# The second block's projection of p moved to the gap between the FFN and that block, and the residuals done on VectorE alone

## The chip, the cores and the metric

The kernel runs on one core of one Trainium2 chip, in one launch. The metric is device time in microseconds: the median of three runs of the kernel before is 2093.15 us (2092.73, 2093.15 and 2098.65). The profile comes from another execution, which took 2099.14 us.

## What is computed

The input is one sequence of 256 tokens with 2048 features; all arithmetic is float32. The first block is an RWKV-7 mixer followed by a convolutional FFN, both under adaptive modulation; the second block is windowed attention beside a short convolution, followed by a gate on a projection of a second input `p` (256 features a token). What matters here, cut from the reference:

```
y, v_first = _rwkv7_mix(h, ...)                       # ends in y @ w_o
x = x + g_m * _rms(y, norm_mix_post)                  # residual 1
h = _rms(x, norm_ffn_pre) * (1 + sc_f) + sh_f
f = _conv_ffn(h, ...)                                 # ends in @ w_out
x = x + g_f * _rms(f, norm_ffn_post)                  # residual 3
# second block
z = rms_norm(x, norm_gain) @ w_in                     # q, k, v, gates, convolution
x = x + mix @ w_out
gate = sigmoid(rms_norm(x, ple_gate_norm_gain) @ w_ple_gate + b_ple_gate)
e = rms_norm(p @ w_ple_proj, ple_norm_gain)           # reads neither x nor z
x = x + gate * e
```

`e` depends on `p` and its weights alone, so `p @ w_ple_proj` can be computed at any time before the last line.

## The kernel before

**Layout.** Activations lie feature-major: 16 tiles (`NT`) of 128 features by 256 tokens (`S`). The residual stream is `xr`, 2 MB.

**Split matmuls.** Every weight tile from `wo` on is split into a high and a low part. ScalarE copies a half unit of weights to `whi` (`hi_part`, L1225), VectorE subtracts to get `wlo` (`lo_part`, L1674), and TensorE multiplies (`split_tiles`, L713 high weights by high and low activations, 512 columns; L714 low weights by high activations, 256 columns). A tile of output takes 16 such pairs. `part_out` (L1232, ScalarE) and `join` (L1682, or L1740 with a scale, VectorE) add the two halves of the bank. Four PSUM banks (0 to 3) take turns; banks 4 to 7 are for side work.

**Phases and the weight ring.** `PHASES` lists the phases in order; here they are `wo` (16 tiles), `fi` (86), `fo` (16, each of three weight units), `zk` (12: keys, queries, values), `zg` (8), `zc` (32), `zo` (16) and `pg` (16). SyncE loads the weight units of 1 MB, in this order, into a ring of four slots; a slot is loaded again when the unit that lay in it is released, which for a split unit is when VectorE has made its low part (`released`).

**Order.** All engines run an order written out by hand and wait on semaphores that count. Each engine and each DMA queue is in order.

**Stage A, from `wo` to `fi`.** TensorE sums the squares of y over partitions (`rms(1)`, L672), ScalarE takes the root (`root`, L1200), VectorE the reciprocal (`rec`, L1714). `residual(1, ...)` then multiplies y by it (four pieces of 128x1024, L1723) and adds it to `xr` (L1727). Pieces 2 and 3 of the multiplication are GpSimd's (`scale_y`, L612); VectorE waits for them (`res_pool`). ScalarE squares each piece of the new x (`squares`, L1194), TensorE sums the squares (16 matmuls, L677), root and reciprocal follow. The new x is multiplied by that (pieces 0 and 1 on VectorE, L1959; 2 and 3 on GpSimd, L618), ScalarE applies scale and shift (L1454), and `split_x` makes high (L1707) and low part (L1708) of each piece. TensorE starts the first half of `fi` when two pieces are split (`x_lo`), and its second half when all four are.

**Stage B, from `fo` to `zk`.** The same residual as `residual(3, ...)`, with x read back from memory into `xy`. ScalarE makes the high part of each of 16 tiles (`scaled_hi`, L1506), VectorE the low part (`scaled_lo`, L1748). TensorE starts the first half of the first tile of `zk` when the low parts 0 to 7 are there, and the second with all 16. ScalarE squares x in four pieces (L1513), GpSimd adds them up (L640, three additions), and TensorE sums over partitions (`after_zk(0)`, L1070) after the first tile of `zk`; root, reciprocal and the scaling of `zk`'s tiles follow, and from the third tile on TensorE does side work for the heads (L1062, L1082).

**Stage C, `zo`.** When the last step of `zc` is done, GpSimd issues two loads of 1 MB, the weights of `p`'s projection, to `wp` (L644), whose place is in use until then. After each of the first eight tiles of `zo` TensorE does a pair of tiles of `p @ w_ple_proj` (8 matmul instructions in the trace, L1163, into bank 4 or 5) in `after_zo`. ScalarE squares the pair (L1615) and copies it to `ee` (L1616), GpSimd adds the squares to `esum`; after tile 9 TensorE sums them, and VectorE scales `ee` in `zo`'s tiles 11 to 14.

Of the kernel before, what the change touches and what calls it, by code (L numbers as in the profile page):

```python
# [29 lines left out]
F32 = mybir.dt.float32  # L30
# [32 lines left out]
          ("zk", 12, 12, 24, 1), ("zg", 8, 8, 16, 1), ("zc", 32, 32, 64, 1),  # L63
# [105 lines left out]
def build(nc, t, out, stage=99, dbg=None):  # L169
    with ExitStack() as ctx:  # L170
# [73 lines left out]
        wp = place("wp", 120, [P, 2, 2048])  # L244
# [85 lines left out]
        res_pool = sem("res_pool")  # L330
        xn_pool = sem("xn_pool")
        zsq_sum = sem("zsq_sum")
        ld_wp = sem("ld_wp")
        e_mm = sem("e_mm")
        e_ev = sem("e_ev")
# [98 lines left out]
        def _(sp):  # L434
# [35 lines left out]
            for name, nu, _, ns, split in PHASES:  # L470
                for k in range(nu):
                    released[RV_UNIT.get((name, k), UNIT[name] + k)] = (w_lo, HALF[name] + 2 * k + 2) if split else \
                        (ada_used, ADA_REST + k + 1) if name == "ada" else (pe_step, STEP[name] + (k + 1) * ns // nu)
# [61 lines left out]
            sp.dma_start(pt[:].rearrange("p i s -> p (i s)"), t["p"]).then_inc(ld_p, 16)  # L535
            stream("zk", t["zin"][0:12], 12)
# [13 lines left out]
        def _(pool):  # L550
# [57 lines left out]
            def scale_y(k, y):  # L608

                pool.wait_ge(rms_rec, k + 1)  # L610
                for q in (2, 3):
                    nc.gpsimd.tensor_tensor(y(q), y(q), rms_rs.unsqueeze(1).to_broadcast([P, 4, S]),  # L612
                                            ALU.mult).then_inc(res_pool, 1)

            scale_y(1, lambda q: cum[:, 4 * q:4 * q + 4, :])
            pool.wait_ge(rms_rec, 3)
            for q in (2, 3):
                nc.gpsimd.tensor_tensor(h[:, 4 * q:4 * q + 4, :], xr[:, 4 * q:4 * q + 4, :],  # L618
                                        rms_rs.unsqueeze(1).to_broadcast([P, 4, S]), ALU.mult).then_inc(xn_pool, 1)

# [14 lines left out]
            scale_y(3, lambda q: xy[:, q, 1])  # L635
# [7 lines left out]
            for k in range(2):  # L643
                pool.dma_start(wp[:, k, :], t["wp"][k]).then_inc(ld_wp, 16)  # L644
            for i in range(NT):
                for e in range(2 * i, 2 * i + 2 if i < 8 else 2 * i):
                    pool.wait_ge(e_ev, i + 1)
# [14 lines left out]
        def _(pe):  # L662
# [58 lines left out]
            def project_split(name, x2, n, between=None, x_rdy=()):  # L721

                def one(k, it):
                    bank_free(TILE[name] + k, it)
                    for x in range(2):
# [3 lines left out]
                        split_tiles(slot, 8, x2, 8 * x, (TILE[name] + k) % BANKS, x == 0, x == 1).then_inc(pe_step, 1)  # L729

# [334 lines left out]

            def after_zk(k):
                if k == 0:
                    pe.wait_ge(zsq_sum, 3)
# [3 lines left out]
                    m.then_inc(rms_sum, 1)  # L1072
                for e in new_heads(k):
# [10 lines left out]
            project_split("zk", x2, 12, after_zk, ((x_lo, 6), (x_lo, 8)))  # L1084
# [66 lines left out]
            def after_zo(k):  # L1151

                if k < 8:
                    if k == 0:
                        pe.wait_ge(ld_wp, 32)
                        pe.wait_ge(ld_p, 16)
                    elif k >= 2:
                        pe.wait_ge(e_ev, k - 1)
                    for e in range(2):
                        i = 2 * k + e  # L1160
                        w = wp[:, i // 8, :].rearrange("p (q m) -> p q m", q=2)
                        for q in range(2):
                            m = mm(ps[:, 4 + k % 2, e * S:(e + 1) * S], w[:, q, (i % 8) * P:(i % 8 + 1) * P], pt[:, q, :],  # L1163
                                   start=q == 0, stop=q == 1)
                    m.then_inc(e_mm, 1)
# [14 lines left out]
        def _(act):  # L1180
# [270 lines left out]
            for i in range(NT):  # L1451
                if i % 4 == 0:
                    act.wait_ge(*((xn_rdy, i // 4 + 1) if i < 8 else (xn_pool, i // 4 - 1)))
# [801 lines left out]
```

## Time and profile before

| | us |
|---|---|
| runs | 2098.65, 2093.15, 2092.73 |
| median | 2093.15 |
| profiled execution | 2099.14 |
| its span, first to last instruction | 2097.5 |
| TensorE matmul busy | 1967.6 (94% of the span) |
| VectorE busy | 1391.2 (66%) |
| ScalarE busy | 896.4 (43%) |
| GpSimd busy | 144.4 (7%) |
| mean granted TensorE clock | 0.968 |
| chain that ended last | TensorE 90%, VectorE 5%, DMA 3% |

The busy shares are means over stages that have different limits. The chain that ended last is followed back from the last instruction; the granted clock is a share of full speed, 1.00 for 2.4 GHz and 0.50 for 1.2 GHz. Where TensorE has nothing to do, a row of another engine stands in the chain. The stages of the change lie at 755 to 797 us (A), 1521 to 1571 us (B) and 1891 to 1960 us (C).

### The profile page before, as it was taken

Reading aid. Unit: us, or ns where it says so; the run is one execution under the profiler, and the core shown is the slowest. Engines: PE = TensorE matmul, PEld = TensorE weight load, DVE = VectorE, ACT = ScalarE, POOL = GpSimd, SP = SyncE. Lnnn points to the kernel's source line nnn. Section 1 sums busy time; section 2 is a strip of 40 time slices with the busy share of each in tenths; the row PEclk is TensorE's granted clock in tenths of the full one; section 3 lists DMA queues with packets and bytes.
Section 4 is the critical chain, followed back from the end, with each engine's and each line's share of the span. In section 5 each row is a group of like instructions: output and inputs, shape, how many; then the busy total and the mean of one; then the engine's idle time right before and its main releaser. Section 6 shows DMA issues by size and latency. Waiting matters only on the chain.

```text
span 2097.5 us, 34270 instructions
## 1 busy us (share of the span) xinstructions
PE 1967.6 (94%) x13392; PEld 1708.1 (81%) x13392; DVE 1391.2 (66%) x1975; ACT 896.4 (43%) x1457; POOL 144.4 (7%) x126
## 2 busy tenths in 40 slices
PE   3999999898998959999999999999959999999999
PEld 2888888787886848888888888888848888887887
DVE  5985459544847977777777776444466567764676
ACT  2335221031333535555555555444444445544553
POOL 2000002000002330000000000000030000002200
PEclk8999999899999979999999999999979999999999
DMA  9986324576645924555555556555524435444453
GB/s 403 413 323 209 121 85 157 201 276 260 243 179 200 409 103 181 193 186 180 185 191 184 182 187 228 184 181 192 192 80 161 161 141 189 153 153 174 158 199 121
DMA packets 58790, 415.14 MB, mean 198 GB/s; under 512 B 6528, under 2 KB 6656, under 8 KB 12416
## 3 DMA queue, kind: packets, MB, share of 16 engines
q1 hardware_dynamic: 54368, 382.24, 49.6%
q0 software_dynamic: 4032, 27.26, 3.3%
q10 hardware_dynamic: 288, 4.19, 0.5%
q8 instruction: 74, 1.21, 0.2%
q14 instruction: 28, 0.23, 0.0%
HBM read 409.48 MB, written 4.19 MB: 197 GB/s over the span
## 4 chain that ended last, share of the span: by engine, by line
PE 90%; DVE 5%; DMA 3%; issue 1%; ACT 1%; POOL 1%; SPq 0%; DVEq 0%; POOLq 0%; ACTq 0%
PE ps L713 41%; PE ps L714 20%; PE ps L690 12%; PE ps L792 4%; PE ps L786 1%; PE ps L772 1%; DMA ring<-in_wv 1%; PE ps L763 1%; DMA bk<-in_ada 1%; PE ps L1163 1%; PE ps L1018 1%; PE ps L808 1%; DVE ring L1652 1%; PE ps L945 1%; POOL zsq L640 1%
## 5 line engine op out<-in xcount | busy, mean ns | idle before, releaser
L713 PE MATMUL ps<-x_pair,whi 128*128 128x512 f32 x2464 | 878.7, 401 | 30.1 <-issue 17.2
L714 PE MATMUL ps<-x_pair,wlo 128*128 128x256 f32 x2464 | 692.8, 281 | 0.0
L1674 DVE TENSOR_TENSOR wlo<-ring,whi 128x1024 fp32r<-128x1024 f32 x468 | 548.2, 1208 | 105.6 <-ACT whi L1225 101.6
L713 PEld LDWEIGHTS ps<-x_pair,whi 128*128 128x128 f32 x2464 | 464.5, 188 | 149.7 <-issue 37.4
L1225 ACT ACTIVATE whi<-ring 128x1024 fp32r<-128x1024 f32 x468 | 462.4, 1031 | 99.7 <-PE ps L714 99.6
L714 PEld LDWEIGHTS ps<-x_pair,wlo 128*128 128x128 f32 x2464 | 467.1, 190 | 0.3
L1232 ACT ACTIVATE px<-ps 128x256 f32<-128x256 f32 x202 | 77.8, 385 | 500.0 <-PE ps L714 500.0
L713 PE MATMUL ps<-hid_pair,whi 128*128 128x512 f32 x688 | 243.3, 399 | 0.0
L714 PE MATMUL ps<-hid_pair,wlo 128*128 128x256 f32 x688 | 193.2, 281 | 0.0
L690 PE MATMUL ps<-mixb,ring 128*128 128x256 f32 x640 | 148.0, 394 | 13.9 <-DMA ring<-in_wv 12.4
L713 PEld LDWEIGHTS ps<-hid_pair,whi 128*128 128x128 f32 x688 | 129.3, 188 | 32.6 <-DVE wlo L1674 0.3
L690 PEld LDWEIGHTS ps<-mixb,ring 128*128 128x128 f32 x640 | 125.9, 198 | 33.7 <-DMA ring<-in_wv 13.4
L1652 DVE CUSTOM_DVE_ANT_0 ring<-ring,cb,prm 128x2048 f32<-128x2048 f32 x42 | 97.6, 2349 | 83.6 <-DMA ring<-in_ada 82.8
L714 PEld LDWEIGHTS ps<-hid_pair,wlo 128*128 128x128 f32 x688 | 130.0, 189 | 0.0
L1682 DVE TENSOR_TENSOR px<-ps,px 128x256 f32<-128x256 f32 x134 | 56.4, 421 | 99.1 <-ACT px L1232 98.8
L690 PE MATMUL ps<-mixa,ring 128*128 128x256 f32 x512 | 115.3, 388 | 0.0
L690 PEld LDWEIGHTS ps<-mixa,ring 128*128 128x128 f32 x512 | 99.3, 195 | 14.4 <-issue 0.2
L1740 DVE TENSOR_TENSOR px<-ps,px 128x256 f32<-128x256 f32 x68 | 28.9, 425 | 122.2 <-ACT px L1232 122.1
L1989 DVE SCALAR_TENSOR_TENSOR tmp<-px,prm,tmp 128x255 f32<-128x255 f32 x86 | 41.6, 484 | 81.5 <-ACT tmp L1478 81.5
L713 PE MATMUL ps<-y_pair,whi 128*128 128x512 f32 x256 | 90.7, 399 | 2.5 <-DVE h L1921 1.4
L792 PE MATMUL ps<-mixb,ring 128*128 128x256 f32 x384 | 85.9, 380 | 0.0
L1478 ACT ACTIVATE tmp<-px,prm 128x256 f32<-128x256 f32 x86 | 51.8, 602 | 70.0 <-DVE px L1682 70.0
(294 smaller groups left out, 2320.5 us busy)
## 6 DMA issues: line engine op xcount, KB each, us to landing
ring<-in_fi SPq DMA_DIRECT2D x86, 1024.0 KB, 4.8
ring<-in_zin SPq DMA_DIRECT2D x52, 1024.0 KB, 4.8
ring<-in_ada SPq DMA_DIRECT2D x42, 1024.0 KB, 6.8
ring<-in_fo SPq DMA_DIRECT2D x32, 1024.0 KB, 4.8
bk<-in_ada SPq DMA_DIRECT2D x22, 1024.0 KB, 10.7
ring<-in_wr SPq DMA_DIRECT2D x16, 1024.0 KB, 4.8
ring<-in_wv SPq DMA_DIRECT2D x16, 1024.0 KB, 4.9
ring<-in_wo SPq DMA_DIRECT2D x16, 1024.0 KB, 8.9
```

The lines of the kernel that those rows point to most:

```text
L690: last = mm(ps[0:m, bank, 0:S], w[:, k * m:(k + 1) * m], act[:, k, :], start=k == 0, stop=k == n - 1)
L713: mm(ps[:, bank, 0:2 * S], w_h, pair_k, start=first and k == 0, stop=False)
L714: m = mm(ps[:, bank, 0:S], w_l, pair_k[:, 0, :], start=False, stop=last and k == n - 1)
L792: last = mm(outer_bank(m), ring[:, i % RING, m * P:(m + 1) * P], mixb[:, i, :], start=i == 0 and m % 2 == 0, stop=i == NT - 1, skip_group_ ...
L1225: A(whi[:, hf % WB, 0:m], ring[:, u % RING, 1024 * x:1024 * x + m], ACT.Copy).then_inc(w_hi, 1)
L1232: A(part[:, (TILE[name] + k) % 4, :], ps[:, (TILE[name] + k) % BANKS, S:2 * S], ACT.Copy).then_inc(x_part, 1)
L1478: A(tmp[:, (k % 4) * S:(k % 4 + 1) * S], join_in("fi", k, it), ACT.Identity, scale=param_at("fcw", 4 * FT, kk), bias=param_at("fcb", 0, kk ...
L1652: V.tensor_tensor_reduce(out=w, in0=w, in1=cb[:], scale=1.0, scalar=prm[:, m:m + 1], op0=ALU.mult, op1=ALU.add, accum_out=mod[:, m:m + 1]) ...
L1674: V.tensor_tensor(wlo[:, hf % WB, 0:m], ring[:, u % RING, 1024 * x:1024 * x + m], whi[:, hf % WB, 0:m].bitcast(F32), ALU.subtract).then_in ...
L1682: return V.tensor_tensor(o, ps[:, (TILE[name] + k) % BANKS, 0:S], o, ALU.add).then_inc(joined, 1)
L1740: own(V.tensor_tensor(o, ps[:, (TILE[name] + k) % BANKS, 0:S], o, ALU.add))
L1989: own(V.scalar_tensor_tensor(d[:, 1:S], b[:, 0:S - 1], param_at("fcw", 2 * FT, kk), d[:, 1:S], ALU.mult, ALU.add))
```

## The change

- The projection of `p` (its eight pairs of tiles) is done around the start of `zk`: pairs 0 to 4 ahead of `zk`, pairs 5 and 6 between the two halves of its first tile (`first_half`), pair 7 after that tile. Three banks (4 to 6) take turns instead of two. The sum of x's squares moves from after `zk`'s first tile to after its second.
- Its weights are two more units of SyncE's ring, phase `pp`, ahead of `zk`; they are released after pair 3 and pair 7. GpSimd's loads of `wp` are gone.
- ScalarE copies each pair to `ee_0` (`p_out`); the whole of it is stored to memory (`spill_e`, 2 MB) in `zk`'s step 1 and loaded by GpSimd to `ee` when `zc` is done. In `zo` ScalarE squares `ee`.
- The pieces of both residuals and of the normalization behind the first that GpSimd did are VectorE's. The splits are in two halves: in A three pieces are normalized, two split, then the fourth normalized and two split; in B three pieces are added, low parts 0 to 7 made, then the fourth added and low parts 8 to 15 made (before: two pieces, four low parts, then the rest).

```diff
-          ("zk", 12, 12, 24, 1), ...
+          ("pp", 2, 0, 0, 0), ("zk", 12, 12, 24, 1), ...
-        wp = place("wp", 120, [P, 2, 2048])
+        ee_0 = place("ee_0", 108, [P, NT, S])
@@ SyncE
-                        (ada_used, ...) if name == "ada" else (pe_step, ...)
+                        (ada_used, ...) if name == "ada" else (e_mm, 4 * k + 4) if name == "pp" else (pe_step, ...)
+            few("pp", [t["wp"][k] for k in range(2)])
             stream("zk", t["zin"][0:12], 12)
@@ GpSimd
-            scale_y(1, lambda q: cum[:, 4 * q:4 * q + 4, :])
-            pool.wait_ge(rms_rec, 3)
-            for q in (2, 3):
-                nc.gpsimd.tensor_tensor(h[:, 4 * q:4 * q + 4, :], xr[:, 4 * q:4 * q + 4, :],
-                                        rms_rs.unsqueeze(1).to_broadcast([P, 4, S]), ALU.mult).then_inc(xn_pool, 1)
-            scale_y(3, lambda q: xy[:, q, 1])
             pool.wait_ge(pe_step, STEP["zo"])
-            for k in range(2):
-                pool.dma_start(wp[:, k, :], t["wp"][k]).then_inc(ld_wp, 16)
+            pool.wait_ge(e_spill, 16)
+            pool.dma_start(ee[:].rearrange("p i s -> p (i s)"), t["spill_e"]).then_inc(ld_e, 16)
@@ TensorE
+                        if first_half and k == 0 and x == 0:
+                            first_half()
+            def p_pair(k):
+                u = UNIT["pp"] + k // 4
+                if k % 4 == 0:
+                    unit_in(u)
+                if k >= 3:
+                    pe.wait_ge(e_ev, k - 2)
+                for e in range(2):
+                    i = 2 * k + e
+                    w = ring[:, u % RING].rearrange("p (q m) -> p q m", q=2)
+                    for q in range(2):
+                        m = mm(ps[:, 4 + k % 3, e * S:(e + 1) * S], w[:, q, (i % 8) * P:(i % 8 + 1) * P], pt[:, q, :],
+                               start=q == 0, stop=q == 1)
+                m.then_inc(e_mm, 1)
             def after_zk(k):
                 if k == 0:
+                    p_pair(7)
+                elif k == 1:
                     pe.wait_ge(zsq_sum, 3)
                     ...
+                if k == 2:
+                    pe.wait_ge(e_ev, 8)
-            project_split("zk", x2, 12, after_zk, ((x_lo, 6), (x_lo, 8)))
+            pe.wait_ge(ld_p, 16)
+            for k in range(5):
+                p_pair(k)
+            def two_pairs():
+                p_pair(5)
+                p_pair(6)
+            project_split("zk", x2, 12, after_zk, ((x_lo, 6), (x_lo, 8)), two_pairs)
             def after_zo(k):
-                if k < 8:
-                    ...
@@ ScalarE
+            def p_out(k):
+                act.wait_ge(e_mm, k + 1)
+                A(ee_0[:, 2 * k:2 * k + 2, :]..., ps[:, 4 + k % 3, :], ACT.Copy).then_inc(e_ev, 1)
+            p_out(0)
             hi_part("zk", 1)
-            for i in range(NT):
-                if i % 4 == 0:
-                    act.wait_ge(x_done, NT + i + 4)
-                scaled_hi(i, "n2")
+            for q in range(4):
+                p_out(q + 1)
+                act.wait_ge(x_done, NT + 4 * q + 4)
+                for i in range(4 * q, 4 * q + 4):
+                    scaled_hi(i, "n2")
             for q in range(4):
                 A(zsq[:, q, :], ..., ACT.Square).then_inc(rms_sq[4], 1)
+                if q < 2:
+                    p_out(5 + q)
@@ in zk's step 1
+                    p_out(7)
+                    act.wait_ge(e_ev, 8)
+                    act.dma_start(t["spill_e"], ee_0[:].rearrange("p i s -> p (i s)")).then_inc(e_spill, 16)
                     root(4)
@@ in zo's steps 1 to 8
-                    act.wait_ge(e_mm, k)
-                    if k >= 3:
+                    if k == 1:
+                        act.wait_ge(ld_e, 16)
+                    elif k >= 3:
                         act.wait_ge(e_acc, 2 * (k - 2))
-                    A(esq[:, (k - 1) % 2], b, ACT.Square)
-                    A(ee[:, 2 * k - 2:2 * k, :], b, ACT.Copy).then_inc(e_ev, 1)
+                    A(esq[:, (k - 1) % 2], ee[:, 2 * k - 2:2 * k, :], ACT.Square).then_inc(e_sq, 1)
@@ VectorE, residual
-                    if q < 2:
-                        V.tensor_tensor(y(q), y(q), ..., ALU.mult).then_inc(sprd, 1)
-                        dve.wait_ge(sprd, 2 * done + q + 1)
-                    else:
-                        dve.wait_ge(res_pool, 2 * done + q - 1)
+                    V.tensor_tensor(y(q), y(q), ..., ALU.mult).then_inc(sprd, 1)
+                    dve.wait_ge(sprd, 4 * done + q + 1)
                     V.tensor_tensor(xr[:, 4 * q:4 * q + 4, :], x(q), y(q), ALU.add).then_inc(x_done, 4)
-                    if q == 1 and k == 3:
+                    if q >= 2 and k == 3:
                         yield
@@ VectorE, from residual 1 to fi
-            for q in range(2):
-                V.tensor_tensor(h...)
-            split_x(h, xhi, xlo, h_rdy, 1 * NT, x_lo)
+            for q in range(3):
+                xn(q)
+            split_x(h, xhi, xlo, h_rdy, 1 * NT, x_lo, (0, 1))
+            xn(3)
+            split_x(h, xhi, xlo, h_rdy, 1 * NT, x_lo, (2, 3))
@@ VectorE, from residual 3 to zk
-            next(halves)
-            for i in range(4):
+            next(parts)
+            for i in range(8):
                 scaled_lo(i, "n2", 0)
-            next(halves)
-            for i in range(4, NT):
+            next(parts)
+            next(parts)
+            for i in range(8, NT):
                 scaled_lo(i, "n2", 0)
```

## Rows read from the trace of the kernel before

**Rows 1.** Waits of TensorE: engine, line, releaser: total us, times, longest us.
```profile
PE ps L677 <- ACT mixb L1194: 24.9, 3, 16.1
...
PE ps L713 <- DVE x_pair L1708: 13.0, 1, 13.0
...
PE ps L1070 <- POOL zsq L640: 6.2, 1, 6.2
...
PE ps L1163 <- DMA wp<-in_wp: 3.2, 1, 3.2
```

**Rows 2.** Chain that ended last, 745 to 800 us: start, us, what.
```profile
759.01 1.24 DVE cum L1723
...
760.34 3.17 DVE mixa L1727
...
768.16 1.06 ACT mixb L1194
...
769.27 7.78 PE ps L677 x24
...
779.36 4.51 DVE h L1959 x2
783.87 2.76 DVE x_pair L1707
...
787.89 0.61 DVE x_pair L1707
```

**Rows 3.** Windows of TensorE: us, busy (instructions), granted clock, DMA share, GB/s.
```profile
764.60:768.50 3.90, 3.78 (x8) 0.50 0.01 2
...
773.00:775.00 2.00, 2.00 (x9) 0.75 0.00 0
...
1545.30:1548.00 2.70, 2.70 (x17) 0.98 0.00 0
```

**Rows 4.** The same chain, 1510 to 1580 us.
```profile
1527.43 1.24 DVE xy L1723
...
1539.30 3.30 ACT x_pair L1506 x8
...
1544.58 5.23 POOL zsq L640
...
1555.62 3.67 PE ps L1070 x8
...
1570.59 0.34 PE ps L1062 x4
```

**Rows 5.** Timelines of single engines, 1500 to 1560 us: start, us, engine, line, operation, [idle before].
```profile
1540.44 4.84 DVE L1748 SCALAR_TENSOR_TENSOR x_pair<-mixa,prm,x_pair 128x256 fp32r<-128x256 f32 x12
...
1544.58 10.99 POOL L640 TENSOR_TENSOR zsq<-zsq 128x1024 f32<-128x1024 f32 x3 [10.44 <-ACT zsq L1513]
...
1542.21 0.77 PE L713 MATMUL ps<-x_pair,whi 128*128 128x512 f32 x1 [17.18 <-issue]
```

**Rows 6.** The same chain, whole span, stretch of zo.
```profile
1901.52 3.78 PE ps L1163 x8
1911.86 1.73 PE ps L1163 x8
...
1955.93 1.73 PE ps L1163 x8
```

**Rows 7.** Timeline of ScalarE, 1890 to 1960 us.
```profile
1905.83 0.59 ACT L1616 ACTIVATE ee<-ps 128x512 f32<-128x512 f32 x1
...
1912.18 2.00 ACT L1225 ACTIVATE whi<-ring 128x1024 fp32r<-128x1024 f32 x2
```

**Rows 8.** DMA issues, 1870 to 1960 us: KB, median us to landing.
```profile
wp<-in_wp POOLq DMA_DIRECT2D x2, 1024.0 KB, 8.1
```

**Rows 9.** DMA issues, 780 to 810 us.
```profile
spill<-mixa ACTq DMA_DIRECT2D x1, 2048.0 KB, 6.2
```

**Rows 10.** DMA issues, 1500 to 1560 us.
```profile
ring<-in_zin SPq DMA_DIRECT2D x6, 1024.0 KB, 4.8
```

More of the change, by code:

```diff
@@ L62 @@
           ("wo", NT, NT, 2 * NT, 1), ("fi", 2 * FT, 2 * FT, 4 * FT, 1), ("fo", 3 * NT, NT, 6 * NT, 1),
-          ("zk", 12, 12, 24, 1), ("zg", 8, 8, 16, 1), ("zc", 32, 32, 64, 1),
+          ("pp", 2, 0, 0, 0), ("zk", 12, 12, 24, 1), ("zg", 8, 8, 16, 1), ("zc", 32, 32, 64, 1),
           ("zo", NT, NT, 2 * NT, 1), ("pg", NT, NT, 2 * NT, 1)]
@@ L329, in build @@
         x_hi = sem("x_hi")
-        res_pool = sem("res_pool")
-        xn_pool = sem("xn_pool")
         zsq_sum = sem("zsq_sum")
-        ld_wp = sem("ld_wp")
         e_mm = sem("e_mm")
+        e_spill = sem("e_spill")
+        ld_e = sem("ld_e")
+        e_sq = sem("e_sq")
         e_ev = sem("e_ev")
@@ L472, in _ @@
                     released[RV_UNIT.get((name, k), UNIT[name] + k)] = (w_lo, HALF[name] + 2 * k + 2) if split else \
-                        (ada_used, ADA_REST + k + 1) if name == "ada" else (pe_step, STEP[name] + (k + 1) * ns // nu)
+                        (ada_used, ADA_REST + k + 1) if name == "ada" else (e_mm, 4 * k + 4) if name == "pp" else (pe_step, STEP[name] + (k + 1) * ns // nu)
             def stream(name, src, n, split=True):
@@ L719, in tiles_of, with project_split @@
                 return lambda k: a[:, k, :, :] if b is None or k < 8 else b[:, k - 8, :, :]
-            def project_split(name, x2, n, between=None, x_rdy=()):
+            def project_split(name, x2, n, between=None, x_rdy=(), first_half=None):
                 def one(k, it):
@@ L1151, in after_zo @@
             def after_zo(k):
-                if k < 8:
[L1154 to L1161, printed above, removed]
-                        for q in range(2):
-                            m = mm(ps[:, 4 + k % 2, e * S:(e + 1) * S], w[:, q, (i % 8) * P:(i % 8 + 1) * P], pt[:, q, :],
-                                   start=q == 0, stop=q == 1)
-                    m.then_inc(e_mm, 1)
                 if k == 9:
@@ L1452, in _ @@
                 if i % 4 == 0:
-                    act.wait_ge(*((xn_rdy, i // 4 + 1) if i < 8 else (xn_pool, i // 4 - 1)))
+                    act.wait_ge(xn_rdy, i // 4 + 1)
                 A(h[:, i, :], h[:, i, :], ACT.Identity, scale=sc1[:, i:i + 1], bias=mod[:, 48 + i:49 + i]).then_inc(h_rdy, 1)
@@ L1543, in _ @@
                     k_ops(11)
+                    act.wait_ge(e_spill, 16)
                 else:
@@ L1957, in _, with xn @@
             rec(2)
-            for q in range(2):
+            def xn(q):
                 V.tensor_tensor(h[:, 4 * q:4 * q + 4, :], xr[:, 4 * q:4 * q + 4, :],
                                 rms_rs.unsqueeze(1).to_broadcast([P, 4, S]), ALU.mult).then_inc(xn_rdy, 1)
-            split_x(h, xhi, xlo, h_rdy, 1 * NT, x_lo)
+            for q in range(3):
[3 more added lines that the diff above has]
+            split_x(h, xhi, xlo, h_rdy, 1 * NT, x_lo, (2, 3))
             s0, t0 = STEP["fi"], TILE["fi"]
@@ L2005, in _ @@
             dve.wait_ge(x_back, 64)
-            halves = residual(3, lambda q: xy[:, q, 1], lambda q: xy[:, q, 0])
-            next(halves)
-            for i in range(4):
+            parts = residual(3, lambda q: xy[:, q, 1], lambda q: xy[:, q, 0])
+            next(parts)
+            for i in range(8):
                 scaled_lo(i, "n2", 0)
-            next(halves)
-            for i in range(4, NT):
+            next(parts)
+            next(parts)
+            for i in range(8, NT):
                 scaled_lo(i, "n2", 0)
@@ L2079, in weights @@
                                     ALU.mult).then_inc(at["pr"], 1)
+            dve.wait_ge(e_spill, 16)
             t0 = TILE["zc"]
@@ L2141, in _ @@
                 if k == 11:
+                    dve.wait_ge(ld_e, 16)
                     rec(5)
@@ L2249 @@
     out = nc.dram_tensor("out_0", (P, NT * S), F32, kind="ExternalOutput").ap()
-    t["spill"] = nc.dram_tensor("spill", (P, NT * S), F32, kind="Internal").ap()
+    for n in ("spill", "spill_e"):
+        t[n] = nc.dram_tensor(n, (P, NT * S), F32, kind="Internal").ap()
     build(nc, t, out)
```

13 lines of the change are left out of this document (4 added, 9 removed).

## The prediction

> **What bounds the kernel now.** I read the table first: TensorE's matmuls are busy for 94% of the span and make up 90% of the chain that ended last. So time can come only from work taken off TensorE, or from its gaps. The waits of TensorE come next [rows 1]; those of five places lie where the change works. In stage A it waits 24.9 us in three pieces for squares of x (one of them, at 764.6, and a short one before 769.27, are this residual's; the longest is from the kernel's start) and 13.0 us for split activations. In B it waits 17.2 us before the first tile of zk [rows 5] and 6.2 us for GpSimd's sum of squares; in C 3.2 us for the load of p's weights. The chain of stage A [rows 2] shows what ends the waits: an addition that takes 3.17 us where its like takes 1.24, and normalization and cast that are slow in the same way (4.51 us for two, 2.76 against 0.61), each while GpSimd does its share of the same step. The windows [rows 3] show the third thing: after each gap the granted clock is 0.50 (1.2 GHz), and it comes back some us later, which costs as much again. I count all three.
>
> The sum is against the profiled execution: span 2097.5 us and 1.6 us around it, 2099.1 us. That execution is 6.0 us above the median of the runs; I subtract the same gain from both and keep the 6 us for the range.
>
> **Stage C: the pairs leave zo.** Removed there: the wait of 3.2 us [rows 1]; pair 0, which runs at the low clock, 3.8 us; seven pairs of 1.73 us, 12.1 us [rows 6]. The tile behind pair 0 lasts from 1905.30 to 1911.86, 6.56 us. A tile at the full clock is the period of the pairs, (1955.93 - 1911.86) / 6 = 7.35, less the pair, 5.62 us. So another 0.9 us goes. Sum: 3.2 + 3.8 + 0.9 + 12.1 = **20.0 us**.
> What is late next? With 5.6 us a tile, ScalarE needs 2.0 us for two high parts [rows 7], 0.6 for the squares and three times 0.4 for single tiles (eight in 3.30 [rows 4]), 3.8 us; VectorE has fewer than that. Neither bounds. The reload of 2 MB stands in GpSimd's queue at the time of the two loads of 1 MB, which took 8.1 us to land [rows 8]; the store of 2 MB took 6.2 us [rows 9]. Landing near 1901.5, it precedes the end of tile 1 (1898.3 + 5.6 = 1903.9), where ScalarE next has to be for TensorE's sake. Behind ScalarE's wait for it stand the copy of tile 1's bank and the high part for tile 3, which TensorE wants at 1909.5, less 2.3 us for high and low part: it may land as late as about 1907 for nothing. Bounds of C: 17 us, if it takes 3 us more than that, to 20.1.
>
> **Stage A: the residual on VectorE alone.** The reciprocal is done at 759.0 [rows 2]. Then four multiplications and four additions at 1.24 us each with GpSimd quiet, with 0.05 us between them: about 2.5 us a piece, the last addition at 769.1 against 770.4, and the first at 761.5 against 763.5. So TensorE's sums of squares start at 762.6 instead of 764.6 (the window begins there [rows 3]), and the last square is ready at 769.1 + 1.06 [rows 2] = 770.2. Four sums take 3.5 to 3.8 us at the low clock and 1.7 at the full one [rows 6]. Before, they were low from 764.6, with a pause, to about 774.0 (clock 0.75 between 773 and 775 [rows 3]), and ended at 777.05. Now they run without a pause. Elsewhere the clock was full again 3.1 us after a gap (1542.2 to 1545.3 [rows 3, 5]) or, behind pair 0, by some 5.7 us. With 5.7, seven sums are done by 768.3 and the rest keep up with the squares: end at 770.2 + 1.7 + 0.4 = 772.3, 4.7 us earlier. If the clock needs 9.4 us from the first sum, as it did before, 5 sums remain at 772.0: end 774.3, 2.7 us earlier.
> Next, normalization and split. Before: from 779.36 to 790.0, 10.6 us. Now: three normalizations 3.8, cast 0.6, low part 1.24, cast, low part, with gaps 7.9 us [rows 2]. Gain 2.7 us. The second half's pieces (one more normalization, two splits) are ready 5.5 us later, and the first half takes 4.5 to 5.1 us at the low clock, so up to 0.5 us may be waited there; before it was the same. Sum of A: 4.7 + 2.7 = **7.4 us**, bounds 5.4 and 7.9.
>
> **Stage B.** The pairs 0 to 4 come into the idle stretch that begins at 1525.03 (1542.21 less 17.18 [rows 5]). At the low clock a pair takes 3.5 us; with the clock back after 3 to 6 us, five are done by about 1535.5. Pair 3 waits for ScalarE's copy of pair 0 (0.6 us [rows 7]) at 1529.5 and pair 4 for that of pair 1, behind two high parts of weights, at 1532.1: both before TensorE gets there. VectorE begins at 1527.43 [rows 4]; three pieces take 7.5 us, to 1535.0; eight low parts at 4.84 / 12 = 0.40 us [rows 5], the last of them behind ScalarE's high parts (four in 1.65 us [rows 4], a copy between the fours; the eighth at 1536.1), end at 1538.4. zk begins there instead of 1542.2. The fourth piece takes VectorE to 1540.8 and the other low parts to 1544.1.
> TensorE's first half takes 5.1 us, if the clock has fallen again in the 3 us since pair 4 (a gap of 3.2 us had it low in C), to 1543.5. Pairs 5 and 6 then cover the wait for the other low parts and end at 1547.3; second half 1550.1, pair 7 1551.9, the second tile 1557.5. Meanwhile ScalarE squares from 1542.5, now with two copies in between (and the waits for pairs 5 and 6), GpSimd adds from about 1546.9 and takes 11.0 us as before [rows 5]: 1557.9. TensorE waits 0.4 us, sums at the full clock in 1.7 instead of 3.7 us [rows 4], and the third tile ends at 1565.3, where before the side work behind it began at 1570.59 [rows 4]: gain 5.3 us. With the clock high through zk's first half it is 1563.5 and 7.1 us. I take **5.7**, near the low-clock case; eight pairs of 1.73 us are thereby hidden.
> The wait for the sum has 5.6 us of cover less than before (one tile instead of two behind it): root, reciprocal, two scaled tiles and ScalarE's operations on them take 4.8 us, so the third tile covers them, with 0.8 us to spare. If that is gone, the loss is what exceeds it.
> SyncE's ring: zk's units 0 and 1 now load where 2 and 3 did, while fo's last tile runs. A load takes 4.8 us [rows 10] and the tile some 15, and until 1538 nobody but ScalarE and VectorE, which idle there, wants the units: I take nothing; the bound is one load, 4.8 us. Unit 2 loads when pair 3 is done, early enough. Unit 3 waits for pair 7 and holds back all behind it: issued at 1551.9, landed by 1557 [rows 10], wanted at 1559. The store of 2 MB starts half a us later; it takes 6.2 us [rows 9] and shares the DMA engines. Cost 0 to 4 us; I take none.
> The Trainium skill (SBUF - State Buffer, section "Who interferes with whom") says that a VectorE instruction with two inputs in SBUF and a GpSimd instruction that reads it exclude each other, and that the loser blocks for the whole of the other's run. The slow rows above agree. For this change it means that the three additions of squares, which now fall among more of VectorE's work, could each be the loser. The first took 5.23 us [rows 4], the three 11.0. Three like the first are 15.7 us: the sum at 1562.6, the third tile's end at 1570.0, and B gives 0.6 instead of 5.7.
>
> **Sum.** 20.0 + 7.4 + 5.7 = 33.1 us, 1.6%: 2066.0 us for the profiled execution, **2060 us** for the median of runs.
>
> **Rivals.**
> 1. The gaps give little: three additions as slow as the first, 9.4 us of low clock in A. Gain 20.0 + 5.4 + 0.6 = 26.0, 2067.1 us. For it: the one addition of 5.23 and the low clock of stage A; against: two of three additions were quick. 0.17.
> 2. The store meets the ring in zk: unit 3 lands 4 us late, ScalarE stands before the tiles' operations, TensorE loses 4 us. Gain 29, 2064 us. 0.10.
> 3. The pairs aren't hidden: TensorE holds zk back for them, 13.8 us for the eight. Gain 33.1 - 13.8 = 19.3, 2074 us. Against: 17.2 us of gap, of which five pairs need 10 to 17. 0.06.
> 4. The other side: the reload holds ScalarE up in zo's step 1, with all high parts behind it. It costs from a landing at 1907 on, one for one, and makes the kernel slower when it eats 33 us and 6 more: landing after 1946, 54 us after issue, where rows of like size have 6.2 and 8.1. 2100 us. 0.02.
> A change that can't be measured (reload 48 us): 0.02.
> The forecast keeps 0.63, with its own range of 2055 to 2066. The range of 8 in 10 takes in rivals 1 and 2 and the 6 us by which the runs before differ among themselves: 2053 to 2069. A measurement of this kernel can tell 0.3% (6.3 us) from no change; all cases but the last two are beyond that: faster 0.95, same 0.03, slower 0.02.
>
> **What would show it.** C: no wait for a load in zo, tiles 5.6 us apart, and no low clock there. A: additions and multiplications of 1.24 us each, sums of squares ending some 15 us after the reciprocal instead of 18, and 8 us from the second reciprocal to fi. B: pairs 0 to 4 within the idle stretch, zk starting 11 us after the first reciprocal instead of 15, no wait of 6.2 us. Wrong if: TensorE's first half of zk starts later than the low parts allow, the three additions take over 13 us, a wait for the ring shows in zk's tile 3, or ScalarE waits for the reload past 1907 on the old scale.

## The result and the profile after

The changed kernel takes 2065.9 us (median of four runs, 2064.8 to 2067.8) where the kernel before takes 2095.9 us (median of four, the three runs known before and one more beside it, 2092.7 to 2101.0): a ratio of 0.986, 95% interval 0.983 to 0.989. The profiled execution took 2064.75 us (span 2063.1), 34.4 us less than the one before. The forecast was 33.1 us less, and 2060 us with a range of 2053 to 2069.

The waits of TensorE first (engine, line, releaser: total us, times, longest). To be seen: those of [rows 1] for GpSimd's sum of squares and for the load in zo are gone, the 13.0 us before fi are 9.9, and the 17.2 us before zk are 4.5.

```profile
PE ps L664 <- ACT mixb L1196: 22.3, 2, 16.2
...
PE ps L700 <- DVE x_pair L1721: 9.9, 1, 9.9
...
PE ps L700 <- issue: 4.5, 1, 4.5
```

**Stage A**, the chain that ended last in the changed kernel (start, us, what). Against [rows 2], additions and normalizations take 1.2 us each, and the 16 sums (32 instructions) run without a pause:

```profile
760.03 1.24 DVE cum L1735
761.36 1.24 DVE mixa L1737
762.62 1.06 ACT mixb L1196
763.73 9.86 PE ps L664 x32
...
775.91 3.50 DVE h L1969 x3
779.40 0.64 DVE x_pair L1720
780.07 1.23 DVE x_pair L1721
...
783.50 0.79 PE ps L700
```

**The clock**, windows of TensorE (us, busy, granted clock, DMA share, GB/s). The reduction of y's squares, behind a wait of 3.0 us, the sums of x's squares, behind one of 6.1, and fi's first half, behind 9.9, begin at 0.50; pairs 0 to 4 run at 1.00 (1514.9 to 1523.6); zk's first half at 0.50 again, after a gap of 4.5 us:

```profile
756.40:757.70 1.30, 1.22 (x2) 0.50 0.00 0
763.70:768.00 4.30, 4.27 (x10) 0.50 0.01 2
768.00:770.00 2.00, 2.00 (x8) 0.71 0.00 0
...
783.50:788.00 4.50, 4.50 (x14) 0.50 0.68 291
...
1514.90:1523.60 8.70, 8.69 (x41) 1.00 0.12 17
1528.10:1533.50 5.40, 5.39 (x17) 0.50 0.00 0
1533.50:1535.50 2.00, 2.00 (x10) 0.93 0.00 0
```

**Stage B**, timeline of TensorE: the five pairs (40 instructions) and zk's first matmul.

```profile
1514.80 8.80 PE L1066 MATMUL ps<-sg,ring 128*128 128x256 f32 x40
1528.11 0.77 PE L700 MATMUL ps<-x_pair,whi 128*128 128x512 f32 x1 [4.52 <-issue]
```

The chain of the same kernel, with the sum of squares (L1076) straight behind zk's second tile and the side work behind the third, then GpSimd's timeline: its additions end at 1545.4, before the sum is due. From zk's first matmul to the side work behind its third tile TensorE doesn't wait at all, so the stage's length is the start of zk plus TensorE's own work at the clock that it is granted.

```profile
1547.29 1.73 PE ps L1076 x8
...
1554.67 0.34 PE ps L1051 x4
```

```profile
1537.12 8.26 POOL L627 TENSOR_TENSOR zsq<-zsq 128x1024 f32<-128x1024 f32 x3 [22.91 <-ACT zsq L1521]
```

The DMA issues between 1530 and 1570 us (KB, median us to landing). The store of 2 MB takes 13.8 us and zk's units 8.4, where they took 6.2 and 4.8 [rows 9, 10]:

```profile
ring<-in_zin SPq DMA_DIRECT2D x7, 1024.0 KB, 8.4
spill_e<-ee ACTq DMA_DIRECT2D x1, 2048.0 KB, 13.8
```

**Stage C**, timeline of ScalarE: its first squares of the reloaded tensor end at 1885.6, and it then waits for TensorE's tile, not for the reload, which landed 9.6 us after it was issued at 1875.40 (the DMA issue below).

```profile
1885.00 0.63 ACT L1629 ACTIVATE esq<-ee 128x512 f32<-128x512 f32 x1
1887.55 0.39 ACT L1234 ACTIVATE px<-ps 128x256 f32<-128x256 f32 x1 [1.92 <-PE ps L701]
```

```profile
ee<-spill_e POOLq DMA_DIRECT2D x1, 2048.0 KB, 9.6
```

In the chain of that stage no pair and no load is left; the sum of e's squares (L1170) comes 57.8 us after zo's start at 1874.94:

```profile
1878.77 0.50 PE ps L700
...
1932.74 0.43 PE ps L1170 x2
```

**Stage lengths.** From here on executions are compared by five stretches, each the difference of two starts or ends in TensorE's timeline: A from the last matmul on `y_pair` to the first on `x_pair`; then the untouched FFN; B from the last matmul on `hid_pair` to the first side work behind zk's third tile (in brackets: from the start of the residual's reciprocal on, which leaves out the 3.9 to 4.4 us between the last matmul of fo and the reciprocal); the untouched rest to zo; C from zo's start to the sum of e's squares.

| profiled execution | A | FFN | B | to zo | C | rest | span |
|---|---|---|---|---|---|---|---|
| before | 37.0 | 731.8 | 48.7 (44.8) | 321.0 | 77.2 | 128.9 | 2097.5 |
| before again | 37.0 | 727.2 | 49.2 (45.3) | 320.9 | 74.8 | 128.9 | 2091.2 |
| changed | 30.1 | 728.2 | 42.8 (38.9) | 320.4 | 57.6 | 130.5 | 2063.1 |
| changed, second | 29.1 | 732.7 | 41.7 (37.8) | 320.2 | 57.6 | 130.4 | 2062.5 |
| changed, third | 30.3 | 719.1 | 42.4 (38.5) | 321.0 | 57.6 | 128.1 | 2052.8 |
| move only | 35.4 | 731.8 | 45.7 (41.8) | 321.0 | 57.6 | 130.4 | 2076.4 |
| residual only | 29.4 | 719.1 | 48.5 (44.6) | 320.3 | 75.2 | 128.8 | 2071.2 |
| no store | 29.2 | 732.7 | 41.7 (37.9) | 321.0 | 56.6 | 128.9 | 2065.9 |
| seven ahead | 30.3 | 719.1 | 42.6 (38.7) | 320.6 | 56.6 | 129.7 | 2055.2 |
| kept busy | 30.2 | 724.5 | 40.7 (36.3) | 320.7 | 57.6 | 130.5 | 2058.9 |
| pairs doubled | 29.1 | 728.2 | 49.3 (45.4) | 320.4 | 57.7 | 130.5 | 2069.2 |
| additions on VectorE | 29.2 | 728.2 | 38.0 (34.1) | 320.3 | 57.6 | 130.5 | 2058.1 |
| the same again | 30.2 | 732.7 | 38.0 (34.1) | 320.6 | 57.7 | 128.1 | 2065.0 |

Between the first two profiles A gave 6.9 us, B 5.9, C 19.6: 32.4 us. The other 2.0 of the 34.4 come from stretches that nothing was done to: the FFN 3.6 shorter, the way to zo 0.5 shorter, the rest 1.6 longer, the start 0.4 longer.

### The profile page after: what moved, and what is told of

It is laid out like the page before. It is cut to its first block, busy times and chain, and to the rows that moved or that the text cites. A ratio compares the mean times of both kernels' runs of the same rounds, so it can differ in the third digit from the quotient of the medians.

```text
span 2063.1 us, 34272 instructions
## 1 busy us (share of the span) xinstructions
PE 1958.8 (95%) x13392; PEld 1703.7 (83%) x13392; DVE 1389.0 (67%) x1981; ACT 897.1 (43%) x1457; POOL 121.3 (6%) x119
## 4 chain that ended last, share of the span: by engine, by line
PE 91%; DVE 4%; DMA 2%; issue 1%; ACT 1%; SPq 0%; POOL 0%; DVEq 0%; ACTq 0%
PE ps L700 41%; PE ps L701 21%; PE ps L677 12%; PE ps L781 4%; PE ps L775 1%; PE ps L761 1%; DMA ring<-in_wv 1%; PE ps L752 1%; DMA bk<-in_ada 1%; PE ps L1007 1%; PE ps L1066 1%; PE ps L797 1%; DVE ring L1665 1%; PE ps L934 1%; PE ps L664 0%
## 5 line engine op out<-in xcount | busy, mean ns | idle before, releaser
L700 PE MATMUL ps<-hid_pair,whi 128*128 128x512 f32 x688 | 238.8, 394 | 0.0
L677 PE MATMUL ps<-mixb,ring 128*128 128x256 f32 x640 | 146.6, 391 | 13.6 <-DMA ring<-in_wv 12.0
L700 PEld LDWEIGHTS ps<-hid_pair,whi 128*128 128x128 f32 x688 | 129.0, 188 | 30.2 <-DVE wlo L1687 0.3
```

The costliest lines, as they stand in the source:

```text
L677: last = mm(ps[0:m, bank, 0:S], w[:, k * m:(k + 1) * m], act[:, k, :], start=k == 0, stop=k == n - 1)
L700: mm(ps[:, bank, 0:2 * S], w_h, pair_k, start=first and k == 0, stop=False)
```

## The experiments

Times stand against the kernel before, run on the same chip in the same series; those of this section are on three chips. Where only one run is given it has no interval.

### Only the move, only the residual

The first undoes the residual's part of the change (GpSimd has its pieces back, the split is the old one); the second makes only that part on the kernel before:

```diff
# move only, against the changed kernel
+            scale_y(1, lambda q: cum[:, 4 * q:4 * q + 4, :])   # GpSimd, and so for 3 and for h
-            for q in range(3):
-                xn(q)
+            for q in range(2):
...
# residual only, against the kernel before: the same lines the other way round
```

> The projection is moved as in the changed kernel, but the residuals and the split are those of the kernel before (GpSimd has its pieces back). Theory 1 (three stages that add up, with B needing both edits): C gives its 19.6 us, A nothing; in B zk still starts 16.6 us after the first reciprocal begins, its first half runs at the low clock, and the third tile of zk ends 42.8 us after the reciprocal begins (before 45.0, changed kernel 38.9), so B gives 2.1. In all 21.7 us: about 2074 us, some 8 to 9 us above the changed kernel. Theory 2 (B's gain comes from the projection's place, which keeps TensorE busy and its clock high): B gives its 5.9 us here too, 2070 us, and the third tile ends within 40 us of the reciprocal.

> The kernel before with the residuals and the normalization on VectorE alone and the splits by halves; the projection stays in zo. Theory 1: A gives its 6.9 us. In B zk starts 3.7 us earlier, but the sum of squares behind its first tile hangs on ScalarE's squares and GpSimd's three additions, which end when they did (30 us after the reciprocal begins), so TensorE's wait there grows from 6.2 to about 9 us and B gives 0 to 1 us. In all 7 to 8 us: 2088 us. Theory 2 (the residual is B's gain): B gives 3.7 us or more, 10.6 in all, 2085 us, with the third tile of zk ending 41 us after the reciprocal begins and the wait for GpSimd's sum still near 6 us.

Move only: 2068.6 us (2064.8 to 2078.1; before 2093.1; ratio 0.988, 0.983 to 0.993). C gives all of its 19.6 us and B 3.0 (from the reciprocal 41.8 instead of 44.8, 42.8 expected). A, where nothing was expected, is 1.6 us shorter with GpSimd's pieces as they were: its sums of squares took 10.1 us instead of 12.4, so A's length varies by that much without the edit. Before zk TensorE still waits 6.9 us behind the five pairs:

```profile
PE ps L716 <- issue: 6.9, 1, 6.9
```

Residual only: 2090.5 us (2072.9 to 2096.8; ratio 0.999, 0.996 to 1.001). The runs show no gain; the median is 2.6 us lower, less than the 7 to 8 us expected. The stages have them: A 7.6 us shorter, B 0.2. (The profiled execution was the fastest of ten, with an FFN of 719.1 us, so its span says nothing of the edit.) TensorE's wait before zk falls from 17.2 to 13.2 us, and that for GpSimd's sum grows from 6.2 to 8.2 (waits of this kernel):

```profile
PE ps L698 <- issue: 13.2, 1, 13.2
PE ps L1055 <- POOL zsq L625: 8.2, 1, 8.2
```

So the shorter residual is worth nothing in B by itself. The sum of squares ends last there, and what it frees turns into a longer wait for that sum. Only with other work behind it (pair 7 and zk's second tile, moved ahead of the sum) does B give 5.9 us: 3.0 from the move, 0.2 from the residual, the rest from both together. Theory 1 holds, theory 2 falls in both.

### The changed kernel again

> The changed kernel once more, as the reference for the others. 2066 us with the same stage lengths: 30.1 us from the last matmul of wo to the first of fi, 38.9 us from the reciprocal to the end of zk's third tile, 57.8 us from zo's start to the sum of e's squares. From fi's start to fo's end, where nothing was changed, it took 3.6 us less than before at the same granted clock. If that is a slow drift of the chip, it differs here by as much, with no tie to the kernel; if it belongs to the kernel, it is 728.2 us again and 731.8 us in the first two runs' untouched parts.

2063.4 us (2059.1 to 2065.2; ratio 0.985, 0.980 to 0.990). A, B and C are within 1.1 us of the first profile. The FFN took 732.7 us, not 728.2: its length isn't the kernel's. B is 1.1 us shorter, most of it in zk's first half, 4.4 us instead of 5.3, in which the clock was not low from the start.

### The store left out

```diff
-                    act.dma_start(t["spill_e"], ee_0[:]...).then_inc(e_spill, 16)
+                    act.sem_inc(e_spill, 16)
-            pool.dma_start(ee[:]..., t["spill_e"]).then_inc(ld_e, 16)
+            pool.dma_start(ee[:]..., t["x"]).then_inc(ld_e, 16)
```

> The changed kernel without the store of the projected p: the reload before zo reads the 2 MB of x instead (so the last addition uses the wrong e). Theory 1 (the store's traffic is hidden): the loads of zk's units land in 5 to 6 us instead of 8.4, no stage changes: 38 to 39 us from the reciprocal to the end of zk's third tile, 320 to 321 us from there to zo, 57.6 us from zo's start to the sum of e's squares. Rival 2 of the prediction (the store holds back the ring and TensorE pays): the stage from the reciprocal to zk's third tile is 2 us or more shorter than the changed kernel's.

One run, 2067.5 us beside 2089.5 before. zk's units land in 5.9 us instead of 8.4 to 8.7 (DMA issues of this kernel):

```profile
ring<-in_zin SPq DMA_DIRECT2D x7, 1024.0 KB, 5.9
```

B is as long as in the changed kernel's second execution (37.9 and 37.8 us from the reciprocal), and the way to zo no shorter (321.0 us), so the store does slow the ring (by 2.5 us a unit) and TensorE doesn't pay. C is 1.0 us shorter, but so it is with seven pairs ahead (below), where the store is in place. In the second execution ScalarE waited 0.7 us for a unit in zk; it had that much to spare. Rival 2 of the prediction named a true collision with no price.

### Seven pairs ahead of zk

```diff
-            for k in range(5):
+            for k in range(7):
                 p_pair(k)
             def two_pairs():
-                p_pair(5)
-                p_pair(6)
+                p_pair(7)
# and p_pair(7) behind zk's first tile is gone
```

> The changed kernel with pairs 0 to 6 ahead of zk and pair 7 between the halves of its first tile (none behind it). Theory 1 (the 4.5 us gap before zk drops the clock, and pairs 5 and 6 then run in the way): the gap shrinks to about 1 us, zk's first half runs at the high clock in 2.8 us instead of 5.4, and the first tile ends some 5 us earlier after the reciprocal; GpSimd's additions then make TensorE wait 1 us. Gain 3.5 to 4 us: 2062 us. Theory 2 (the gap's clock doesn't matter, since the other low parts and the sum of squares end last): the sum of squares starts when it did, within 1 us, and the time is 2065 to 2066 us, no change.

2060.8 us (2056.1 to 2071.7; ratio 0.986, 0.980 to 0.992), B 38.7 us from the reciprocal: nothing gained. The first half of theory 1 came true: the gap before zk is 1.1 us, and zk's first half runs at 1.00 and takes 2.9 us. Theory 2 falls too, for the sum of squares starts 1.9 us earlier than in the first profile (29.6 us after the reciprocal begins instead of 31.6). But behind the second tile TensorE now waits 2.6 us for GpSimd's additions, which take 10.5 us instead of 8.3, and the sum and the beginning of the third tile run at 0.50. The waits, GpSimd's timeline and TensorE's windows of this kernel:

```profile
PE ps L1074 <- POOL zsq L627: 2.6, 1, 2.6
...
PE ps L700 <- issue: 1.1, 1, 1.1
```

```profile
1528.66 10.47 POOL L627 TENSOR_TENSOR zsq<-zsq 128x1024 f32<-128x1024 f32 x3 [20.46 <-ACT zsq L1518]
```

```profile
1521.60:1525.60 4.00, 3.50 (x19) 1.00 0.00 0
1539.60:1541.60 2.00, 2.00 (x9) 0.71 0.96 365
1541.60:1543.60 2.00, 2.00 (x8) 0.50 0.96 406
```

The single instructions of this trace show where GpSimd's time goes. Its first addition starts while VectorE makes two low parts, one behind the other; those take their usual 1.23 us, the addition 3.65. The second takes 3.40 beside another low part of 1.23. VectorE's next low part starts while that addition runs, takes 3.42 us, and ends 1.1 us behind it. In the changed kernel two additions started with VectorE idle, and took 2.40 and 2.37 us. So an operation that starts while the other engine's runs lasts longer by about the rest of that one. Three additions of 2.4 us, with their gaps, would have ended 0.4 us before TensorE wanted the sum (an estimate from these figures).

### The additions of squares on VectorE

```diff
# GpSimd
-            for q in range(1, 4):
-                ...
-                nc.gpsimd.tensor_tensor(zsq[:, 0, :], zsq[:, 0, :], zsq[:, q, :], ALU.add).then_inc(zsq_sum, 1)
# VectorE, behind lo_part("zk", 1); the rest as in the run before
+            for q in range(1, 4):
+                dve.wait_ge(rms_sq[4], q + 1)
+                if q > 1:
+                    dve.wait_ge(zsq_sum, q - 1)
+                V.tensor_tensor(zsq[:, 0, :], zsq[:, 0, :], zsq[:, q, :], ALU.add).then_inc(zsq_sum, 1)
```

> Seven pairs ahead of zk and pair 7 in the middle of its first tile, as in the run before, and now the three additions of squares on VectorE behind its low part of zk's second unit, instead of GpSimd. There GpSimd's additions took 10.5 us, TensorE waited 2.6 us and fell to the low clock for the third tile. Theory 1 (two engines at one port were the reason): the additions take 1.24 us each, end before the second tile does, no wait and no low clock follow, and the time from the reciprocal to the end of zk's third tile falls from 38.7 to about 34 us. Theory 2 (ScalarE's squares are what ends last): the additions end as late, and it stays at 37 us or more.

B is 34.1 us from the reciprocal, as theory 1 had it: 4.6 less than in the run before, from which only the additions' engine differs, and 2.2 to 4.8 less than in the executions with the changed kernel's B. VectorE's timeline has the three additions in 3.9 us:

```profile
1535.95 3.87 DVE L2027 TENSOR_TENSOR zsq<-zsq 128x1024 f32<-128x1024 f32 x3
```

The edit removes two things at once, the collision with VectorE's low parts and GpSimd's own pace (2.4 us an addition alone, against 1.24). By the estimate above the first is what made TensorE wait.

The time is 2061.2 us (2046.5 to 2063.8; ratio 0.986, 0.980 to 0.991). It was run again beside the changed kernel:

> The changed kernel again, as the reference of the next run: about 2064 us, 30 us less than before; from the reciprocal to the end of zk's third tile 36.3 to 39 us, by where the clock falls.

> The kernel with seven pairs ahead of zk and the additions of squares on VectorE again, in more rounds. Theory (only the stage between the blocks is shorter, by 4 us): 34.1 us from the reciprocal to the end of zk's third tile, a median 4 us below the changed kernel's of the same call, 2060 us, if the spread of the untouched stretch lets it be seen. Rival: the gain is taken back later, and the medians are equal with a longer stretch from there to zo.

Changed kernel 2058.3 us (2052.4 to 2073.6; ratio 0.986, 0.983 to 0.989), this one 2064.1 us (2055.7 to 2066.7; 0.986, 0.984 to 0.988). B was 34.1 us again, with the way to zo no longer than before, so the rival falls. Yet the medians point the other way: the FFN alone took 732.7 us here and 719.1 in the changed kernel's profiled execution. The shorter B is shown by the profiles; that this version beats the changed kernel in time is not.

### TensorE kept busy before fi

```diff
             rms(2, mixb)
+            for _ in range(5 * 4):
+                mm(ps[:, 4, 0:S], const("ones").to_broadcast([P, P]), const("sin"), start=True, stop=True)
```

> The changed kernel with 20 matmuls of 128x256 whose result nobody reads, behind the sums of squares of residual 1, in the 9.9 us in which TensorE waits for the first split activations of fi. Theory: they take 8.6 us at the high clock, fi starts 9.9 us after the sums as before, and its first 4.5 to 5.5 us at the low clock become high: the first tile is 2.0 to 2.6 us shorter. Rival: the clock falls anyway, or the additions make fi start late; then the first tile is as long, or fi starts more than 10 us after the sums, and nothing is gained.

2063.3 us (2059.1 to 2071.7; ratio 0.990, 0.985 to 0.994). The fillers take 8.8 us, fi starts on time and at the high clock, but its first tile ends no sooner: ScalarE takes it out 9.8 us after fi's start, where it was 8.7 and 8.4 us in two executions of the changed kernel. TensorE is through the first half early and waits 2.1 us for the second half's activations, after the fillers' 1.3 us, and the clock falls to 0.57 behind that (timeline, then windows):

```profile
774.76 8.80 PE L1035 MATMUL ps<-cst 128*128 128x256 f32 x40
784.84 0.49 PE L700 MATMUL ps<-x_pair,whi 128*128 128x512 f32 x1 [1.29 <-DVE x_pair L1723]
...
789.98 0.49 PE L700 MATMUL ps<-x_pair,whi 128*128 128x512 f32 x1 [2.10 <-DVE x_pair L1723]
```

```profile
784.80:790.80 6.00, 3.86 (x21) 1.00 0.72 306
790.80:792.80 2.00, 2.00 (x9) 0.57 0.35 139
792.80:794.80 2.00, 2.00 (x9) 0.58 0.00 0
```

The low clock before fi had cost next to nothing: the first half at 0.50 lasts 5.3 us, and the other two pieces are ready 5.0 us after fi's start in either kernel. The theory falls; nothing is gained, as the rival had it, and the tile is even 1.1 to 1.4 us longer, with the low clock in its second half.

The same execution shows what the low clock costs in B. Pairs 0 to 4 ran their first 5 us at it here, where nothing waits for them, ended later, and left a gap of 2.0 us before zk; the clock stayed at 1.00 through it (timeline, then a window):

```profile
1526.31 0.47 PE L700 MATMUL ps<-x_pair,whi 128*128 128x512 f32 x1 [2.01 <-issue]
```

```profile
1525.80:1527.80 2.00, 1.49 (x9) 1.00 0.47 197
```

zk starts 12.5 us after the reciprocal begins in all executions with this B, and TensorE doesn't wait behind it. Only the first half differs, and with it the stage:

| profiled execution | gap before zk | pairs 0 to 4 | zk's first half | B from the reciprocal |
|---|---|---|---|---|
| changed | 4.5 | 8.8 | 5.3 | 38.9 |
| changed, third | 4.5 | 8.8 | 5.0 | 38.5 |
| changed, second | 2.8 | 10.5 | 4.4 | 37.8 |
| no store | 2.8 | 10.5 | 4.4 | 37.9 |
| kept busy | 2.0 | 11.4 | 2.9 | 36.3 |

Stage less first half is 33.4 to 33.7 us each time. So the low clock before zk is paid for almost whole, up to 2.4 us in the first half and 2.7 in the stage. With pairs 5 and 6 behind it, the first half doesn't end in a wait for the other low parts, as fi's does.

### The pairs doubled

```diff
-                    for q in range(2):
+                    for q in range(4):      # q % 2 in the operands: each product twice
```

> The changed kernel with every pair of p's projection computed twice over (the same result), 13.8 us more work for TensorE at the high clock. Theory 1 (pairs lie in waits): pairs 0 to 4 overfill the gap by 4.2 us, but zk's first half then runs at the high clock, and the whole costs about half of the added work: from the reciprocal to the end of zk's third tile 45 to 46 us instead of 38.9. Theory 2 (whatever TensorE does here is paid for): 52 to 53 us.

One run, 2070.9 us. B from the reciprocal is 45.4 us, 6.5 more than in the first profile of the changed kernel, for 13.8 us of added work; zk starts 16.3 us after the reciprocal begins instead of 12.5, all at the full clock. Theory 1 holds, about half of the added work is paid. The other half didn't all fall into waits: the five pairs ahead of zk add 8.7 us and delay it by 3.8; the three behind its start add 4.9 and are paid whole; and zk's first half, with no gap before it, takes 3.0 us instead of 5.3, which gives 2.2 back.

### The kernel before again

> The kernel before, once more, for its stage lengths. If the length of the untouched stretch from fi's start to fo's end belongs to the execution and not to the kernel, it is one of the values seen so far with other kernels (719.1, 724.5, 728.2, 731.8 or 732.7 us), with equal chance of being other than the 731.8 us of this kernel's first profile. Stages A, B and C are 36 to 37, 48 to 49.5 and 75 to 78 us.

One run, 2092.9 us; the FFN took 727.2 us, a value between. C took 74.8 us, 2.4 less than in the first profile: the load landed earlier, TensorE waited 1.9 us for it instead of 3.2, and pair 0 ran at a mean clock of 0.64 instead of 0.50 and took 3.0 us instead of 3.8 (chain of this execution):

```profile
1888.60 7.68 DMA wp<-in_wp
1896.32 3.00 PE ps L1163 x8
```

## Why the prediction was right

**C, 20.0 forecast, 19.6 between the profiles.** The terms were a wait, pair 0, a slowed tile and seven pairs. The second profile of before shows that the first three (8 us) aren't fixed: by it C gives 17.2, so that 19.6 lies within half a us of the forecast is owed to the execution from which the terms were read. The reload landed 10.1 us after zo's start, as forecast (1901.5 less 1891.4), without holding ScalarE up: its squares start 0.1 us behind its operation before and end at 1885.6, 1.9 us before the tile that it waits for next (1887.55).

**A, 7.4 forecast, 6.9.** The residual with the sums, from the reciprocal's start on: 15.3 us (758.25 to 773.59) instead of 19.8, 4.5 for the forecast 4.7; the clock came back some 5.4 us after the first sum (0.71 between 768 and 770), close to the shorter of my two cases, 5.7. Normalization and split, from the second reciprocal to fi: 9.4 instead of 12.4, 3.0 for 2.7. Missed: the reduction of y's squares ran at the low clock this time (1.24 us for 0.71), and with its wait that takes 0.6 back. Over all profiles A is 35.4 to 37.0 us without this part of the change and 29.1 to 30.3 with it, 5.1 to 7.9 us apart, so the half us between forecast and result tells nothing. That the low clock in fi's first half just covers the way to the other two pieces was right, and it is why the fillers bought nothing.

**B, 5.7 forecast, 5.9.** zk starts 12.5 us after the reciprocal begins (12.8 forecast), and its first half ran at the low clock, as assumed. The third tile ends 38.9 us after it (39.7). The intermediate steps were less good: pairs 0 to 4 ran at the full clock in this execution (8.8 us, against about 10 forecast) and partly at the low one in the second (10.5 us), and the additions took 8.3 us instead of 11.0, so the wait that I had foreseen for them didn't come. Neither miss moved the sum much. VectorE's first eight low parts set zk's start (they end 12.4 us after the reciprocal begins), and behind it TensorE works without a wait; the additions end 1.8 us before the sum is due. That the result lies so near rests on the clock: by the executions above this B gives from 5.9 us, with the low clock in zk's first half, to 8.5 with the high one (44.8 less 38.9 to 36.3), where my two cases were 5.3 and 7.1. I took 5.7, near the low one, and the first profile has the low clock.

**The port rule.** Three additions each losing to VectorE, the case that stood beside the Trainium skill's page SBUF — State Buffer, section "Who interferes with whom", was given 0.17 (with A's low clock). In the changed kernel they took 8.3 us, less than the 15.7 worked out from the first, since two of them met an idle VectorE. But it did decide once TensorE was ahead: 10.5 us, a wait and a clock drop with seven pairs ahead, all gone when GpSimd no longer took part. The rows agree with that section's rule in size and direction: who starts second lasts longer by about the rest of the other's operation (GpSimd 3.65 and 3.40 us for 2.4, VectorE 3.42 for 1.23). That it is the shared port on which they wait stands in no row.

**The other rivals.** The store's collision was real and free. Of the pairs, the five ahead of zk were hidden. The three behind its start are 5.2 us of TensorE's work in a stretch without a wait, so they were not hidden as the prediction had it: with two of them moved ahead of zk and the additions on VectorE, B is 2.2 us shorter at the same clock (34.1 for 36.3), and a wait of 0.9 us for low parts comes in. The reload had 1.9 us in hand.

**The sum.** 33.1 us against 34.4 between the profiled executions and 30.0 between the medians. The predicted 2060 us was 6 us under the measured median: 2.7 of that is the median of before, 2095.9 in the comparison instead of 2093.2, and 3.1 is the gain. The latter is within what the FFN alone does from one execution to the next. The time by itself would not decide between the forecast and its rivals 1 (2067.1) and 2 (2064), for the median is 2065.9; the stages do. And the prediction's 0.3% for what a measurement can tell was too fine: the kernel before spread over 2082.8 to 2102.3 us, 0.9%, in one series.

## What to carry to other kernels

Independent work belongs in front of the wait that ends last, not only where an engine is free: the residual alone gave B 0.2 us, the move alone 3.0, both 5.9. Price a low clock by what comes behind the slowed work: before fi it was nearly free, since the next input came just as late; before zk, with work at hand that needs no input, it cost up to 2.7 us. Look at how far two engines' operations overlap before giving one of them a share of the other's work. When a change is worth less than the untouched stretches vary, compare stage lengths from several profiles instead of medians.

## What the runs showed that I had not expected

TensorE's matmuls run at two slightly different rates at one and the same granted clock of 1.00. Windows of 20 us in fi (900) and fo (1400) hold 115 or 116 instructions, or 117 (columns as above; in order: before, changed, seven ahead):

```profile
900.00:920.00 20.00, 20.00 (x116) 1.00 0.52 191
1400.00:1420.00 20.00, 20.00 (x115) 1.00 0.55 189
```

```profile
900.00:920.00 20.00, 20.00 (x115) 1.00 0.53 198
1400.00:1420.00 20.00, 20.00 (x117) 1.00 0.58 193
```

```profile
900.00:920.00 20.00, 20.00 (x117) 1.00 0.56 184
1400.00:1420.00 20.00, 20.00 (x117) 1.00 0.59 193
```

One phase keeps one rate: the pair of matmuls takes 0.353 us all through fi and 0.347 all through fo in the changed kernel, both slow in the first profile of before, both quick with seven ahead. The FFN takes 719.1 us at the quick rate and 731.8 to 732.7 at the slow one, 728.2 and 724.5 or 727.2 with a mixture, in kernels whose FFN is the same. That makes up to 13.6 us (1.9% of the stretch), where the runs of the kernel before spread over 19.5 us in one series (2082.8 to 2102.3 us); that it explains most of that spread is not shown, for the other runs have no profile. The rate changes from one execution to the next on one and the same chip. What chooses it is open; it wasn't tried.
